# Feed-forward rows turned on VectorE by 32x32 blocks and gathered by transfers within SBUF

## What is computed

```
D_MODEL = 1024; SEQ = 256; D_FF = 2816
def swiglu(h, w_gu, w_down):
    g, u = jnp.split(h @ w_gu, 2, axis=-1)
    return (jax.nn.silu(g) * u) @ w_down

# first block, twice; the second block adds a modulated gate gt and a norm behind it
x = x + 0.5 * swiglu(rmsnorm(x, ffn1_norm[i]), ffn1_wgu[i], ffn1_wdown[i])
...
mods = (jax.nn.silu(c) @ w_ada[l] + b_ada[l]).reshape(B, N_MOD, 1, D_MODEL)
```

## Time and profile before

| | us |
|---|---|
| median of 3 runs (1356.0 to 1356.04) | 1356.03 |
| span of the profiled execution | 1354.2 |
| what lies around that span, by the median | 1.8 |
| TensorE busy | 1339.0 |
| VectorE busy | 930.6 |
| ScalarE busy | 749.4 |

### The profile page before, as it was taken

How to read it: one execution, slowest core, us unless ns; L and a number is a source line. 1 busy time by engine, 2 the same in 40 slices (tenths; PEclk the granted TensorE clock), 3 DMA queues, 4 the chain that set the end, 5 groups by cost and what they waited for, 6 DMA issues and landing times.

```text
span 1354.2 us, 17190 instructions
## 1 busy us (share of the span) xinstructions
PE 1339.0 (99%) x6599; PEld 1117.7 (83%) x6599; DVE 930.6 (69%) x1334; ACT 749.4 (55%) x1169; POOL 67.2 (5%) x132
## 2 busy tenths in 40 slices
PE   9999999999999999999999999999999999999998
PEld 6888888888888888888788888889988888788886
DVE  6677867856656777877767787678866455755553
ACT  6444448567864544446845444766457664744442
POOL 3100100000000000010000010100000000000000
PEclk9999999999999999999999999999999999999999
DMA  9888866543376678885577885665544355556662
GB/s 282 290 262 277 310 199 190 167 117 108 100 243 195 214 252 272 289 288 167 168 245 250 279 290 150 202 173 159 168 140 112 108 172 169 166 180 184 187 190 88
DMA packets 167057, 270.89 MB, mean 200 GB/s; under 512 B 14242, under 2 KB 114826, under 8 KB 166976
## 3 DMA queue, kind: packets, MB, share of 16 engines
q1 hardware_dynamic: 154240, 226.66, 53.8%
q0 software_dynamic: 12576, 43.06, 9.5%
q10 hardware_dynamic: 160, 0.07, 0.0%
HBM read 268.66 MB, written 1.05 MB: 199 GB/s over the span
## 4 chain that ended last, share of the span: by engine, by line
PE 94%; DVE 3%; ACT 1%; DMA 1%; issue 0%; POOL 0%; DVEq 0%; SPq 0%; ACTq 0%
PE ps L1982 25%; PE ps L1947 16%; PE ps L1949 16%; PE ps L1948 16%; PE ps L2171 2%; PE ps L1961 1%; PE ps L2182 1%; PE ps L1962 1%; PE ps L1963 1%; PE ps L2065 1%; PE ps L2067 1%; PE ps L2066 1%; PE ps L2488 1%; PE ps L1997 1%; PE ps L2086 1%; PE ps L2255 1%
## 5 line engine op out<-in xcount | busy, mean ns | idle before, releaser
L1151 DVE TENSOR_TENSOR w_lo<-raw,w_hi 128x1024 fp32r<-128x1024 f32 (+2 forms) x431 | 515.1, 1214 | 249.1 <-ACT w_hi L636 246.9
L636 ACT ACTIVATE w_hi<-raw 128x1024 fp32r<-128x1024 f32 (+2 forms) x431 | 448.5, 1054 | 330.5 <-DMA raw<-in_ffn_wgu_dram 92.8
L1947 PE MATMUL ps<-w_hi,a_hi 128*128 128x512 f32 (+1 forms) x976 | 390.5, 400 | 1.1 <-DVE w_lo L1151 0.8
L1949 PE MATMUL ps<-w_hi,a_lo 128*128 128x512 f32 (+1 forms) x976 | 379.5, 389 | 0.0
L1948 PE MATMUL ps<-w_lo,a_hi 128*128 128x512 f32 (+1 forms) x976 | 378.5, 388 | 0.0
L1949 PEld LDWEIGHTS ps<-w_hi,a_lo 128*128 128x128 f32 x976 | 183.3, 188 | 38.8
L1947 PEld LDWEIGHTS ps<-w_hi,a_hi 128*128 128x128 f32 x976 | 183.6, 188 | 36.1 <-DVE w_lo L1151 1.0
L1948 PEld LDWEIGHTS ps<-w_lo,a_hi 128*128 128x128 f32 x976 | 183.8, 188 | 34.6
L1982 PE MATMUL ps<-w_hi,hid_hi 128*128 128x512 f32 x300 | 93.5, 393 | 0.0
L1982 PE MATMUL ps<-w_lo,hid_hi 128*128 128x512 f32 x300 | 92.5, 390 | 0.0
L1982 PE MATMUL ps<-w_hi,hid_lo 128*128 128x512 f32 x300 | 92.5, 390 | 0.0
(11 more groups left out here) (433 smaller groups left out, 1640.4 us busy)
## 6 DMA issues: line engine op xcount, KB each, us to landing
raw<-in_ffn_wgu_dram SPq DMA_DIRECT2D x176, 256.0 KB, 4.2
raw<-in_w_in_dram SPq DMA_DIRECT2D x88, 512.0 KB, 3.7
raw<-in_w_gu_dram SPq DMA_DIRECT2D x176, 256.0 KB, 3.3
ada<-in_w_ada_dram POOLq DMA_DIRECT2D x72, 512.0 KB, 5.4
raw<-in_ffn_wdown_dram SPq DMA_DIRECT2D x44, 512.0 KB, 4.6
raw<-in_w_dn_dram SPq DMA_DIRECT2D x44, 512.0 KB, 4.3
raw<-in_w_in_dram SPq DMA_DIRECT2D x36, 256.0 KB, 3.1
raw<-in_w_out_dram SPq DMA_DIRECT2D x16, 512.0 KB, 4.1
```

Source lines behind the costliest of these rows:

```text
L636: act.activation(w_hi[:, u % RING, 0:nk * n], raw[:, u % RING, 0:nk * n], ACT.Copy).then_inc(hi_ready, 1)
L1151: dve.tensor_tensor(w_lo[:, u % RING, 0:nk * n], raw[:, u % RING, 0:nk * n], w_hi[:, u % RING, 0:nk * n].bitcast(F32), ALU.subtract).then_ ...
L1947: pe.matmul(dst(t)[:, 0:n], a[0], slot(u, w_hi, kk, n), start=kc == 0, stop=False)
L1949: i = pe.matmul(dst(t)[:, 0:n], a[1], slot(u, w_hi, kk, n), start=False, stop=kc == KC - 1)
```

## The change

`hid` loses its double buffer. After each iteration's product VectorE turns `hid` by 32x32 blocks (`turn_blocks`): rows within each group of 32 partitions are exchanged with 32 columns, into `turned_even` or `turned_odd`, by turns per pair of iterations. A pair is a group m, six in a feed-forward, the last one of a single iteration. What is still missing is the exchange between the four quarters of partitions. SP does it with 16 transfers a group (`gather_hidden`), partition quarter i of `turned` to quarter q of `gathered`, four each ahead of four loads in a row, the first ahead of unit 4*(2m+2)+11. `gathered` is single: group m+1 is gathered once `hid_lo` of group m is written. `hidden_hi` and `hidden_lo` work on a group, from `gathered`, at j = 2m+3 behind the next two units; those of the last two groups come in `w_down`, behind units dn+9 and dn+13. `turn_hidden` is gone. `first_down` waits for `hid` in two steps. The POOL load of `ple_norm`, whose place `turned_odd` shares, waits until the second feed-forward's last group is gathered.

```diff
@@ -219,3 +219,6 @@
         sg, _, e = place("sg", [P, 2, T, HALF], F32, HB)
-        hid, _, END = place("hid", [P, 2, T, HALF], F32, e)
+        hid, _, e = place("hid", [P, T, HALF], F32, e)
+        turned_even, _, END = place("turned_even", [P, T, 4, 4, 32], F32, e)
+        turned_odd, _, _ = place("turned_odd", [P, T, 4, 4, 32], F32, B0 + 4096)
+        gathered, _, _ = place("gathered", [P, T, 4, 4, 32], F32, KD0)
         assert END <= nc.sbuf_usable_end, (END, nc.sbuf_usable_end)
@@ -291,2 +294,5 @@
 
+        def turned(m):
+            return turned_odd if m % 2 else turned_even
+
         def wide(t):
@@ -417,2 +423,3 @@
         FFN = ["f0", "f1", "f2", "f3"]
+        HGROUPS = (UPB + 1) // 2
 
@@ -524,2 +531,20 @@
 
+            def gather_hidden(f, m, i):
+
+                nh = 2 * min(2, UPB - 2 * m)
+                g = HGROUPS * f + m
+                if i == 0:
+                    sp.wait_ge(sem("blocks_turned"), f * UPB + min(2 * m + 2, UPB))
+                    if g >= 1:
+                        sp.wait_ge(sem("hid_lo_ready"), g)
+                for q in range(4):
+                    sp.dma_start(gathered[32 * q:32 * q + 32, :, i, 0:nh, :], turned(m)[32 * i:32 * i + 32, :, q, 0:nh, :])\
+                      .then_inc(sem("hid_gathered"), 16)
+
+            gather_at = {}
+            for f in range(4):
+                for m in range(HGROUPS):
+                    for i in range(4):
+                        gather_at[ffn[f][0] + 4 * min(2 * m + 2, UPB) + RING + 3 + i] = (f, m, i)
+
             xs = A["x"][0].rearrange("(t p) d -> p t d", p=P)
@@ -530,2 +555,4 @@
             for u in range(XQ, NU):
+                if u in gather_at:
+                    gather_hidden(*gather_at[u])
                 load_unit(u)
@@ -611,5 +638,6 @@
             pool.dma_start(pin[:, :, :], A["p"][0, 0].rearrange("(t p) d -> p t d", p=P)).then_inc(sem("pin_landed"), 16)
-            load_ada(ADA_F + 3, ADA_F + 9)
+            load_ada(ADA_F + 3, 2 * ADA_F)
+            pool.wait_ge(sem("hid_gathered"), 256 * 2 * HGROUPS)
             pool.dma_start(grow[:, :], A["ple_norm"][0].partition_broadcast(P)).then_inc(sem("grow_landed"), 16)
-            load_ada(ADA_F + 9, 2 * ADA_F + 3)
+            load_ada(2 * ADA_F, 2 * ADA_F + 3)
             load_brow(2)
@@ -779,6 +807,6 @@
                         act.activation(csil[:, :], par[:, :, ROW[("c_2", 0)]], ACT.Silu).then_inc(sem("csil_ready"), 1)
-                    if j >= 1:
-                        hidden_hi(f, j - 1)
                     if j < UPB - 1:
                         w.to(up + 4 * j + 8)
+                    if j >= 3 and j % 2 == 1:
+                        hidden_hi(f, j // 2 - 1)
                     act.wait_ge(used, up + 4 * j + 4)
@@ -789,4 +817,6 @@
                                        scale=rstd[:, t:t + 1] if f < 2 else 1.0).then_inc(sem("silu_ready"), 1)
-                w.to(dn + 5)
-                hidden_hi(f, UPB - 1)
+                w.to(dn + 8)
+                hidden_hi(f, HGROUPS - 2)
+                w.to(dn + 12)
+                hidden_hi(f, HGROUPS - 1)
                 if f >= 2:
@@ -799,6 +829,7 @@
 
-            def hidden_hi(f, j):
-                act.wait_ge(sem("hid_turned"), f * UPB + j + 1)
-                act.activation(hid_hi[:, 2 * j:2 * j + 2, :].rearrange("p c n -> p (c n)"), ps[:, 4 + j % 2, :], ACT.Copy)\
-                   .then_inc(sem("hid_hi_ready"), 1)
+            def hidden_hi(f, m):
+                n = 2 * min(2, UPB - 2 * m)
+                act.wait_ge(sem("hid_gathered"), 256 * (HGROUPS * f + m + 1))
+                act.activation(hid_hi[:, 4 * m:4 * m + n, :].rearrange("p c (g u) -> p c g u", u=32),
+                               gathered[:, :, :, 0:n, :].rearrange("p t i c u -> p c (t i) u"), ACT.Copy).then_inc(sem("hid_hi_ready"), 1)
 
@@ -1370,4 +1401,2 @@
                         dve.tensor_copy(maskD[:, :], const[:, C_D:C_D + P]).then_inc(sem("mask_ready"), 1)
-                    if j >= 1:
-                        hidden_lo(f, j - 1)
                     take_mods(FFN[f], j - 1)
@@ -1377,12 +1406,15 @@
                         w.to(up + 4 * j + 8)
+                    if j >= 3 and j % 2 == 1:
+                        hidden_lo(f, j // 2 - 1)
                     for t in range(T):
                         dve.wait_ge(sem("silu_ready"), 2 * (f * UPB + j) + t + 1)
-                        if j >= 2:
-                            dve.wait_ge(sem("hid_turned"), f * UPB + j - 1)
+                        if f + j > 0:
+                            dve.wait_ge(sem("blocks_turned"), f * UPB + j)
                         if f < 2:
-                            i = dve.scalar_tensor_tensor(hid[:, j % 2, t, :], acc(t, j % 2)[:, HALF:], rstd[:, t:t + 1],
+                            i = dve.scalar_tensor_tensor(hid[:, t, :], acc(t, j % 2)[:, HALF:], rstd[:, t:t + 1],
                                                          sg[:, j % 2, t, :], ALU.mult, ALU.mult)
                         else:
-                            i = dve.tensor_tensor(hid[:, j % 2, t, :], sg[:, j % 2, t, :], acc(t, j % 2)[:, HALF:], ALU.mult)
+                            i = dve.tensor_tensor(hid[:, t, :], sg[:, j % 2, t, :], acc(t, j % 2)[:, HALF:], ALU.mult)
                     i.then_inc(sem("hid_ready"), 1)
+                    turn_blocks(f, j)
                     if f < 3 and j in (6, 10):
@@ -1390,3 +1422,2 @@
                 w.to(dn + 5)
-                hidden_lo(f, UPB - 1)
                 for n in range(4):
@@ -1395,2 +1426,7 @@
                     w.to(dn + 8 + 3 * n)
+                    if n == 0:
+                        hidden_lo(f, HGROUPS - 2)
+                    if n == 1:
+                        w.to(dn + 12)
+                        hidden_lo(f, HGROUPS - 1)
                     if n == 1:
@@ -1403,6 +1439,19 @@
 
-            def hidden_lo(f, j):
-                dve.wait_ge(sem("hid_hi_ready"), f * UPB + j + 1)
-                dst, hf = (b[:, 2 * j:2 * j + 2, :].rearrange("p c n -> p (c n)") for b in (hid_lo, hid_hi))
-                dve.tensor_tensor(dst, ps[:, 4 + j % 2, :], hf.bitcast(F32), ALU.subtract).then_inc(sem("hid_lo_ready"), 1)
+            def turn_blocks(f, j):
+
+                c = 2 * (j % 2)
+                dve.wait_ge(sem("hid_ready"), f * UPB + j + 1)
+                g = HGROUPS * f + j // 2
+                if j % 2 == 0 and g >= 2:
+                    dve.wait_ge(sem("hid_gathered"), 256 * (g - 1))
+                for t in range(T):
+                    i = dve.transpose(turned(j // 2)[:, t, :, c:c + 2, :], hid[:, t, :].rearrange("p (c q u) -> p q c u", c=2, u=32))
+                i.then_inc(sem("blocks_turned"), 1)
+
+            def hidden_lo(f, m):
+                n = 2 * min(2, UPB - 2 * m)
+                dve.wait_ge(sem("hid_hi_ready"), HGROUPS * f + m + 1)
+                dst, hf = (b[:, 4 * m:4 * m + n, :].rearrange("p c (g u) -> p c g u", u=32) for b in (hid_lo, hid_hi))
+                dve.tensor_tensor(dst, gathered[:, :, :, 0:n, :].rearrange("p t i c u -> p c (t i) u"), hf.bitcast(F32), ALU.subtract)\
+                   .then_inc(sem("hid_lo_ready"), 1)
 
@@ -2128,4 +2177,2 @@
                             ins.then_inc(sem("par_turned"), 1)
-                        if j >= 1 and i == (2 if j == 1 else 1):
-                            turn_hidden(f, j - 1)
                         if i == 3:
@@ -2133,4 +2180,2 @@
                 for k in range(FC - SKEW):
-                    if k == 2:
-                        turn_hidden(f, UPB - 1)
                     if f == 1 and k == 8:
@@ -2138,3 +2183,2 @@
                         pe.wait_ge(sem("pin_landed"), 16)
-                        pe.wait_ge(sem("hid_lo_ready"), f * UPB + UPB)
                         for c in range(2):
@@ -2143,3 +2187,3 @@
                         i.then_inc(sem("pin_turned"), 1)
-                    pe.wait_ge(sem("hid_lo_ready"), f * UPB + k // 2 + 1)
+                    pe.wait_ge(sem("hid_lo_ready"), HGROUPS * f + k // 4 + 1)
                     if k < 2:
@@ -2153,3 +2197,3 @@
                         sum_mods(FFN[f], UPB + 1)
-                pe.wait_ge(sem("hid_lo_ready"), f * UPB + UPB)
+                pe.wait_ge(sem("hid_lo_ready"), HGROUPS * f + HGROUPS)
                 if f == 2:
@@ -2162,4 +2206,3 @@
                 for n in (1, 0):
-                    if n == 0:
-                        pe.wait_ge(sem("hid_ready"), f * UPB + UPB)
+                    pe.wait_ge(sem("hid_ready"), f * UPB + UPB - n)
                     for k in range(2):
@@ -2175,11 +2218,2 @@
 
-            def turn_hidden(f, j):
-                pe.wait_ge(sem("hid_ready"), f * UPB + j + 1)
-                if j >= 2:
-                    pe.wait_ge(sem("hid_lo_ready"), f * UPB + j - 1)
-                for c in range(2):
-                    for t in range(T):
-                        i = pe.transpose(ps[:, 4 + j % 2, c * S + t * P:c * S + (t + 1) * P], hid[:, j % 2, t, c * P:(c + 1) * P], ident)
```

(2 more changed lines are left out.)

## The result

The changed kernel takes 1385.26 us (median of 4 runs, 1380.8 to 1388.11) against 1356.01 in the same comparison: a ratio of 1.0215, with a 95% interval of 1.0194 to 1.0235. It is 29 us **slower**. The forecast was 1344.5, faster, in a range up to 1353.5. So the sum missed 41 us, and what came is neither the forecast nor one of the rivals as they were told.

A forecast was written before the change was run, and what follows sets the result against it. TensorE, busy 99% of the span, was taken to bound the kernel. 1354.2 us less 20.7 for the turns plus 9.1 given back is 1342.6, with 1.8 to the median 1344.4, forecast as 1344.5; range 1334 to 1353.5.

The forecast's parts named there:

- What TensorE gets back: TensorE in the four feed-forwards: 44 turns removed at 0.47 us each, a gain of 20.7 us.
- VectorE: VectorE in inner rows: 88 block transposes at 0.43 us, about 85% busy in the first feed-forward; it keeps up.
- ScalarE "nothing", covered by more than 5 us: ScalarE's copies of gathered cost nothing; silu starts up to 1.2 us later, covered by more than 5 us.
- SP: SP's queue: four gathers at 0.37 us ahead of a load make 2.3 us in a unit of 2.72 us; it fits.
- rival C: SP becomes the bound: at 1.08 us a gather, 22 pairs of iterations lose 49 us, 1384 us; chance 0.08.
- the gate sum: After w_down unit 14 in feed-forwards 1 to 3: TensorE waits 2.9, 1.1 and 2.6 us for m_lo.
- the knot: SP's last-group gather waits for hidden_lo, delaying loads 11 to 13: 1 us in each of three feed-forwards, ends 0 and 3.
- Part of the delay is absorbed: Unit 13's load in w_down leaves 3 to 5 us later, but it had queued, so part of that is absorbed.
- B: DMA fills up to 0.97 to 1.05 in the inner rows: 1351.5 us; chance 0.12 together with a longer knot on SP.
- A: The wait at the gate sum does not come, so 20.7 us stay: 1335.3 us; chance 0.20.
- D: The turns' time was hidden under a wait, so the time stays 1356 us; chance 0.05 with what ends beside it.
- The rule weighed in C: Transfers under 64 KB are dominated by their descriptors; the 2.5 us landing of a 16 KB transfer was set against it.

The follow-up runs named there:

- no_turn: The kernel before without the 44 turns on TensorE, high and low parts taken straight from hid: 1334.42 us, ratio 0.985.
- blocks_only: The kernel before with the change's 88 block transposes added on VectorE, into a buffer nobody reads: 1355.11 us, ratio 1.0002.
- hid_ahead: The changed kernel, last group in its own buffer, its parts later, hid ahead of the products at the last j, gate sum behind unit 16: 1340.41 us.
- gathers_only: The kernel before with the change's 384 transfers added at the same places of SP's queue, into a buffer nobody reads: 1393.21 us, ratio 1.0281.
- spread_two_buffers: The kernel before with 384 unused transfers added, two ahead of each of eight loads, into two buffers by turns: 1357.41 us, ratio 1.0013.
- last_buffer_alone: The changed kernel with only each feed-forward's last group gathered into a buffer of its own, ScalarE's and VectorE's order kept: 1365.14 us, ratio 1.0078.
- gathers_tiny: The kernel before with the 384 unused transfers added in bursts of four, each carrying 32 bytes a row instead of 512: 1388.16 us, ratio 1.0237.

## Why the prediction was wrong

**What TensorE gets back** was right: 20.6 us measured against 20.7 (no_turn). The working from the spacing of the weight loads held, and the 272 ns of a transpose's row would have promised 48.

**VectorE** was right: 0.424 us a block transpose against 0.43, and free (blocks_only).

**ScalarE "nothing", covered by more than 5 us**, was not tested by itself. ScalarE did wait for the gathers, 29.3 us in all ahead of `hid_hi`, and `hid` came late at `first_down`, 8.4 + 1.6 us, a place that the sum did not have. The products ahead of `hid` in VectorE's order are a part of that: with them moved behind it (hid_ahead), 0.2 us of waits for `hid` are left there.

**SP was the step that failed.** "I take 0.37 each: 1.5 + 0.84 = 2.3 us in a unit of 2.72 us. It fits." It was 0.597 each, 2.4 to 2.5 us for four, and the load behind them went from 0.84 to 1.05 us: with the short gaps in between 3.7 us a unit and up to 4.5. It does not fit. The figure came from another form of transfer, half a unit with 256 rows, and from the cheaper half: the earlier trace rows show 0.367 us only as the minimum of line 523, whose median is 0.471. A dearer gather stood only in rival C, with a chance of 0.08. The sum was made from the average too: C asked from which issue time SP is full over a pair of iterations (0.94 us), and at 0.6 it is not. But a ring of eight slots feels the four units of the burst, not the mean of eight. For the inner rows the experiments show it: 17.6 us of waits for `hid` with bursts of four (gathers_only), 2.6 with pairs (spread_two_buffers). For the whole +38 against +2 us they don't, since gathers_only also stops SP in `w_down`; and the changed kernel itself with its gathers in pairs was not run.

**The place of the loss was right, its size was not.** The prediction named the gate sum in FFN 1 to 3, the longer chain on VectorE ahead of it, and the knot on SP. It gave the gate sum 2.9, 1.1 and 2.6 us, and 1 us each for the knot "with 0 and 3 as ends": 9.1. The waits were 30.2, and with the low clock behind them more. The 3 us for the knot are the second term that was mis-sized: without it (last_buffer_alone) the kernel is 20 us faster. The knot was sized from a kernel whose loads left on time. In fact `hid_lo` of that group ended at 154.45, not at 151.0, since its own gathers and the copy ahead of it were late as well (3.16 us idle before it); then SP put 2.5 us of gathers ahead of each load that was already late. Unit 13 was copied at 168.82 instead of the 161.60 that the sum started from. From that copy's end to the gate sum the prediction had 17.4 us and the trace has 19.4, 2.4 of which is a wait for `ada`: the chain itself was sized well, its start was not. "Part of the delay is absorbed" was right: unit 13's load left at 164.08 instead of 153.61, 10.5 us later, and its copy started 7.2 us later. But 3.3 us absorbed are little against 10.5; the prediction had counted on a delay of 3 to 5. SP's row of that load in the kernel before:

```profile
153.61 0.33 SPq L519 DMA_DIRECT2D raw<-in_ffn_wdown_dram  x1
```

**The low clock** was not in the sum. Between the kernel after and no_turn it makes up to 13.7 of the 54.2 us; how much of the 13.7 is the clock was not worked out stretch by stretch.

**The rivals.** C came nearest in time (1384), by accident: its mechanism, SP full over a whole pair at 1.08 us a gather, did not occur. B saw the DMA engines fuller, and they were (a share of 0.98 from 60 to 100 us, where it was 0.79 and 0.88), but that is not the loss: a sixteenth of the bytes still cost 33 us, and spread_two_buffers lost 2 us at 0.88 to 1.02. A did not come, since the gate sum waited, and no_turn rules out D. The rule weighed in C, that small transfers are dominated by their descriptors, is one that the Trainium skill, "DMA: Bandwidth & Descriptors", section "Bandwidth", gives with figures of loads from HBM issued by GpSimd. The traces agree in so far as the time to landing hardly follows the bytes: a median of 3.2 us with 32 KB (gathers_only) and 2.9 with 2 KB (gathers_tiny). But what was dear here is the time on the issuing queue, not the transfer.

**What stays open.** Why hid_ahead, with its bursts, loses only 6 us against no_turn, while the kernel before with the same bursts loses 38, is only argued: the kernel before stops for `hid` in the middle of the inner rows at each turn, has the gate sum two units earlier, and its added gathers stop SP in `w_down`. On that reading a burst at 0.6 us an issue does harm only where the order around it leaves no slack; no run shows it by itself. And why a transfer of 64 rows takes longer to issue than one of 256 was not tried; all that had 0.6 us touch 32 partitions at a time on at least one side.
